# A two-part transformer step on one core: the mixing layer's modulation, spatial mix and output product rebuilt in turned form

## The reference, cut to what matters

```python
def modulate(x, g, shift, scale):
    return rmsnorm(x, g) * (1 + scale) + shift

    sh1, sc1, gt1, sh2, sc2, gt2 = adaln(c, w_mod, b_mod)    # silu(c) @ w_mod + b_mod, six vectors of 1024
    csh1, csc1, ... = adaln(c_ctx, w_mod, b_mod)
    hl, hc = modulate(xl, g_mix, sh1, sc1), modulate(xc, g_mix, csh1, csc1)
    # 8 query heads of 64 in 2 groups (q_gain, rotation), keys and values of both hl and hc: 256 x 512 scores a head
    # spatial gating: u, vv = split(gelu(h @ w_gm)); vv = rmsnorm(vv); w_s is 8 groups of 128 x 128 over rows
    mixed = einsum('gij,bcjgd->bcigd', w_s, vv) + b_s.T[:, :, None];  return u * mixed
    xl_new = xl + gt1 * (concat([attention, gating]) @ w_out)
    xl_new = xl_new + gt2 * expert_choice_ffn(modulate(xl_new, g_ffn, sh2, sc2), w_router, w1, w3, w2)
```

## Time and profile before

| | us |
|---|---|
| executions of the kernel, median of 3 | 1479.61 (1477.10 to 1479.96) |
| profiled execution, its own time | 1483.23 |
| its span, first to last instruction | 1481.4 |
| busy: PE, DVE, ACT, POOL | 1009.3, 333.3, 249.5, 131.7 |
| HBM read, mean rate | 479.66 MB, 324 GB/s over the span |
| granted TensorE clock, mean | 0.845 |

### The profile page before, as it was taken

The page is one execution under the profiler, slowest core; times in us unless marked ns, Lnnn a source line. Parts: engine busy times, 40 slices in busy tenths (PEclk is TensorE's granted clock), DMA queues, the critical chain, the costliest instruction groups (busy, mean ns, idle before and its releaser), DMA issues.

```text
span 1481.4 us, 14254 instructions
## 1 busy us (share of the span) xinstructions
PE 1009.3 (68%) x6208; PEld 497.8 (34%) x6208; DVE 333.3 (23%) x749; ACT 249.5 (17%) x511; POOL 131.7 (9%) x102
## 2 busy tenths in 40 slices
PE   4979857665656556566565565656666688789976
PEld 1855642221211111111111111111111687679875
DVE  3854440000010000000000000000000648445561
ACT  2532311000000000000000000000000645434451
POOL 1320300000100000000000000000000462300032
PEclk9989779989877888787888887787878899889988
DMA  9856358999999999999999999999999141234401
GB/s 386 302 217 226 150 227 334 428 427 428 427 428 429 428 427 428 427 429 428 428 428 427 429 427 428 427 428 428 428 428 423 60 171 58 90 138 158 165 20 43
DMA packets 38340, 481.64 MB, mean 325 GB/s; under 512 B 6577, under 2 KB 7662, under 8 KB 9222
## 3 DMA queue, kind: packets, MB, share of 16 engines
q1 hardware_dynamic: 37126, 476.53, 77.2%
q10 hardware_dynamic: 832, 3.15, 0.5%
q0 software_dynamic: 320, 1.05, 0.2%
HBM read 479.66 MB, written 1.05 MB: 324 GB/s over the span
## 4 chain that ended last, share of the span: by engine, by line
DMA 56%; PE 29%; DVE 8%; ACT 4%; issue 1%; POOL 1%; SPq 0%; DVEq 0%; POOLq 0%; ACTq 0%
DMA ring<-in_t_w 55%; PE PS L466 8%; PE PS L901 4%; PE PS L478 4%; PE PS L947 2%; DMA ring<-in_t_mod 2%; PE PS L456 2%; PE PS L649 1%; ACT S L591 1%; DVE RR L437 1%; PE PS L744 1%; PE PS L835 1%; PE PS L772 1%; ACT RR L431 1%; DVE S L606 1%
## 5 line engine op out<-in xcount | busy, mean ns | idle before, releaser
L901 PE MATMUL PS<-ring,S 128*32 128x512 f32 x2048 | 316.2, 750 | 224.9 <-DMA ring<-in_t_w 223.4
L947 PE MATMUL PS<-ring,S 128*32 128x512 f32 x1024 | 174.9, 817 | 114.2 <-DMA ring<-in_t_w 108.3
L901 PEld LDWEIGHTS PS<-ring,S 128*32 128x32 f32 x2048 | 62.6, 124 | 468.0 <-DMA ring<-in_t_w 346.5
L466 PE MATMUL PS<-RR,SR 128*128 128x512 f32 (+3 forms) x520 | 144.0, 398 | 14.5 <-DVE RR L627 6.6
L437 POOL TENSOR_TENSOR RR<-ring,RR 128x1024 fp32r<-128x1024 f32 (+2 forms) x43 | 94.8, 2232 | 267.9 <-ACT RR L431 267.2
L947 PEld LDWEIGHTS PS<-ring,S 128*32 128x32 f32 x1024 | 33.9, 131 | 238.6 <-DMA ring<-in_t_w 159.2
L466 PEld LDWEIGHTS PS<-RR,SR 128*128 128x128 f32 x520 | 99.9, 197 | 39.8 <-DVE RR L627 7.3
L486 ACT ACTIVATE S<-PS 128x512 f32<-128x512 f32 (+3 forms) x60 | 33.6, 568 | 388.4 <-PE PS L456 338.1
L456 PE MATMUL PS<-KC,S 128*128 128x128 f32 (+1 forms) x378 | 59.8, 309 | 46.5 <-DVE S L1346 13.0
L431 ACT ACTIVATE RR<-ring 128x1024 fp32r<-128x1024 f32 (+3 forms) x95 | 89.2, 1003 | 9.9 <-DMA ring<-in_t_in_kv 6.0
L1699 ACT ACTIVATE S<-PS 128x512 f32<-128x512 f32 x16 | 9.6, 597 | 474.0 <-PE PS L901 474.0
(11 more groups left out here) (275 smaller groups left out, 935.8 us busy)
## 6 DMA issues: line engine op xcount, KB each, us to landing
ring<-in_t_w SPq DMA_DIRECT2D x192, 2048.0 KB, 31.5
ring<-in_t_mod SPq DMA_DIRECT2D x12, 2048.0 KB, 11.2
ring<-in_t_out SPq DMA_DIRECT2D x6, 2048.0 KB, 7.6
ring<-in_t_e_g SPq DMA_DIRECT2D x2, 2048.0 KB, 8.4
ring<-in_t_o_q SPq DMA_DIRECT2D x2, 2048.0 KB, 7.4
ring<-in_t_o_k SPq DMA_DIRECT2D x2, 2048.0 KB, 7.5
ring<-in_t_o_v SPq DMA_DIRECT2D x2, 2048.0 KB, 7.5
ring<-in_t_o_g SPq DMA_DIRECT2D x2, 2048.0 KB, 7.4
```

Source lines behind the costliest of these rows:

```text
L466: m = pe.e.matmul(PS[:, b, 0:width], l_, r_, start=(k == 0 and n == 0), stop=(k == k8 - 1 and n == 2))
L901: m = pe.e.matmul(PS[32 * j:32 * j + 32, b, :], XE[:, 2 * k + kk, 32 * e_:32 * e_ + 32], place[name, e_, k][:, kk, 512 * j:512 * j + 512], ...
L947: m = pe.e.matmul(PS[q:q + 32, b, :], HT[e_ % 2][:, 128 * s + 32 * j:128 * s + 32 * j + 32], place["w2", e_, j][:, s, 512 * dh:512 * dh + ...
```

## The change

- **Modulation by halves.** w_mod is cut in 12 units of one vector's 512 columns (all 1024 rows, eight matmuls). ACT copies the row, four matmuls with a two-column selector turn it (`mod_cols`, L742), and DVE adds bias and gain (`mod_col`). Scale and shift of columns 0 to 511 come first, then kv over those, then scale and shift of the rest, then kv's second half. DVE modulates x and ctx together, with one residue for both; ACT makes both high parts.
- **Ring.** Order: sc1 and sh1 of half 0, kv, sc1 and sh1 of half 1, q, vv, u, six units of gt1, sc2, sh2, w_out in two units, gt2 in two, experts.
- **Attention.** u by `straight`; w_s comes turned from memory and its mixing result turned. Probabilities are divided by their sum on DVE before they are transposed, so that the values stay stationary: eight matmuls of 64 × 256 for two passes. Mixing and attention results go straight to `MT`'s parts. High parts and residues of w_out are made within passes 5 to 8.
- **Router stage.** The output product by `straight`, into x turned (`XT`, 1 MB from memory), gt1 a column scalar; logits from this turned x1 with w_router times the scale; mean squares by matmul; x1 turned back by 16 transposes; both gt2 units ahead of the affinity transposes; the first gather takes one expert, four more follow (`GROUPS`). `g_final` is fetched among the experts.
- **Small inputs.** One transfer of 806 KB instead of 552.5 KB and some twenty small ones and a transpose.

```diff
+MODS = [(n, h) for pair in (("sc1", "sh1"), ("gt1",), ("sc2",), ("sh2",), ("gt2",)) for h in range(2) for n in pair]
...
+    mod_unit("sc1", 0, 0)
+    mod_unit("sh1", 0, 1)
+    in_unit("kv", 256, 2, 2, 2048)
+    mod_unit("sc1", 1, 3)
+    mod_unit("sh1", 1, 4)
+    in_unit("q", 512, 5, 6)
+    in_unit("vv", 512, 0, 1)
+    in_unit("u", 512, 3, 4)
+    for n, slot in zip(MODS[4:10], (2, 5, 6, 0, 1, 2)):
+        mod_unit(*n, slot)
+    for h, slot, hslot in ((0, 5, 6), (1, 3, 4)):
+        unit(("out1", h), unit_rows(f"t_out1_{h}", 8, 512), 8, 512, slot, hslot)
+    mod_unit("gt2", 0, 0)
+    mod_unit("gt2", 1, 1)
+    SLOTS = (2, 5, 6, 3, 4, 0, 1)
...
             if key == ("in", "u"):
-                sp.e.dma_start(wr[:], kview(A["w_router"])).then_inc(*landed("w_router"))
-                sp.e.dma_start(sinkb[:], A["e_sinks_2"].partition_broadcast(P)).then_inc(*landed("sinks"))
-                sp.e.dma_start(bfb[:], A["o_b_f_2"].partition_broadcast(P)).then_inc(*landed("b_f"))
-                sp.e.dma_start(wf[:], kview(A["o_w_in_2"])[:, :, 3072:3088]).then_inc(*landed("wf"))
+                sp.wait_ge(("xn", 0), ("xn", 1))
+                sp.e.dma_start(XT, A["t_xT"].rearrange("p (k t) -> p k t", k=8)).then_inc(*landed("xT"))
...
+        def mod_part(name, h):
+            key, w = ("mod", name, h), place[name, h]
+            b = banks.take(key, ALL6)
+            pe.wait_ge(banks.was[key], ("cv", 0), ("cv", 1), ("load", (name, h)))
+            for k in range(8):
+                q = k % 4
+                m = pe.e.matmul(PS[32 * q:32 * q + 32, b, :], cvec[:, k, :], w[:, k, :], start=k < 4, stop=k >= 4)
+            m.then_inc(*pe.mark(used((name, h)), key))
+        def mod_cols(name, h):
+            key = ("col", name, h)
+            b = banks.take(key, ALL6)
+            pe.wait_ge(banks.was[key], out_of(("mod", name, h)))
+            row = bm[:, MODS.index((name, h)) % 3, :]
+            for s in range(4):
+                m = pe.e.matmul(PS[:, b, 2 * s:2 * s + 2], row[:, 128 * s:128 * s + 128], quarters[:, 0:2], start=True,
+                                stop=True)
+            m.then_inc(*pe.mark(key))
...
+        mod_part("sc1", 0)
         pe.wait_ge(*[("xn", i) for i in range(4)])
         for k in range(8):
             transposes(pe, ("raw", k), ALL6, [(XN if i < 2 else XC)[:, i % 2, 128 * k:128 * k + 128] for i in range(4)])
-        mod_part(0, 2)
-        mod_part(0, 3)
-        mod_cols(0)
+        mod_cols("sc1", 0)
+        mod_part("sh1", 0)
+        mod_cols("sh1", 0)
         for i in range(4):
             banks.take(("kv", i), ALL6, hold=True)
+            pe.wait_ge(banks.was["kv", i])
+        kv_part(range(4))
+        mod_part("sc1", 1)
+        mod_cols("sc1", 1)
+        mod_part("sh1", 1)
+        mod_cols("sh1", 1)
+        kv_part(range(4, 8))
         for i in range(4):
-            pe.wait_ge(banks.was["kv", i])
             banks.release(("kv", i))
-        for k in range(8):
-            pe.wait_ge(("h", k), ("split", ("in", "kv"), k))
-            for i in range(4):
-                for n, (l_, r_) in enumerate(products(("in", "kv"), (HI[:, i // 2], LO[:, i // 2]), k, slice(0, 256),
-                                                      slice(128 * (i % 2), 128 * (i % 2) + 128))):
-                    m = pe.e.matmul(PS[:, banks.of["kv", i], 0:256], l_, r_, start=(k == 0 and n == 0),
-                                    stop=(k == 7 and n == 2))
-        m.then_inc(*pe.mark(("kv", 0), ("kv", 1), ("kv", 2), ("kv", 3), used(("in", "kv"))))
         for i in range(2):
...
+            for n2 in range(2):
+                straight(pe, ("u", n2), ("in", "u"), HL, n2, final=n2 == 1)
                 yield
             for i in range(2):
                 b = banks.take(("mixed", i), ALL6)
-                pe.wait_ge(banks.was["mixed", i], out_of(("wst", 0)), out_of(("wst", 1)), ("vn", 0), ("vn", 1))
+                pe.wait_ge(banks.was["mixed", i], ("load", "w_s"), ("vn", 0), ("vn", 1))
                 for g in range(8):
-                    m = pe.e.matmul(PS[:, b, 64 * g:64 * g + 64], WST[:, g, :], VV[:, i, 64 * g:64 * g + 64], start=True,
-                                    stop=True)
+                    m = pe.e.matmul(PS[64 * (g % 2):64 * (g % 2) + 64, b, 128 * (g // 2):128 * (g // 2) + 128],
+                                    VV[:, i, 64 * g:64 * g + 64], WST[:, g, :], start=True, stop=True)
                 m.then_inc(*pe.mark(("mixed", i)))
                 yield
-            for G in (1, 2):
-                for k in range(4):
-                    mod_part(G, k)
-                    yield
+            for n, part_ in enumerate(A1_MODS):
+                mod_part(*part_)
+                if n:
+                    mod_cols(*A1_MODS[n - 1])
+                yield
+            mod_cols(*A1_MODS[-1])
+            yield
 
...
+                    pe.wait_ge((1, "p", n - 1, g))
...
+            if n and n % 2 == 0:
+                batch, i = n // 2 - 1, (n - 1) // 4
+                if batch % 2 == 0:
+                    banks.take((1, "o", i), (OB[i],))
+                    pe.wait_ge(banks.was[1, "o", i])
+                pe.wait_ge(out_of(("kv", 3)), *[out_of((1, "t", m_, g)) for m_ in (n - 2, n - 1) for g in range(2)])
+                for s in range(4):
+                    for g in range(2):
+                        m = pe.e.matmul(PS[64 * g:64 * g + 64, OB[i], 256 * (batch % 2):256 * (batch % 2) + 256],
+                                        KV[:, s, 128 + 64 * g:192 + 64 * g], PTB[batch % 2][:, s, g, :], start=s == 0,
+                                        stop=s == 3)
+                m.then_inc(*pe.mark((1, "pv", batch), *([(1, "o", i)] if batch % 2 else [])))
         rest(side)
...
+        pe.wait_ge(("mixt", 0), ("mixt", 1), ("MT", 0), ("MT", 1))
+        for n2 in range(4):
+            straight(pe, ("out1", n2), ("out1", n2 // 2), MT, n2 % 2, final=n2 % 2 == 1, ks=(4, 5, 6, 7, 0, 1, 2, 3))
+            if n2:
+                logits(n2 - 1)
+        pe.wait_ge("sqa")
+        mean_square(sqa, True)
+        logits(3)
+        pe.wait_ge(("sq", 3))
+        mean_square(sq2[0], False)
+        for i in range(2):
+            banks.release(("logits", i))
+        for i in range(2):
+            for h in range(2):
+                transposes(pe, ("x1t", i, h), ALL6, [XT[:, 4 * h + k, 128 * i:128 * i + 128] for k in range(4)])
+        mod_part("gt2", 0)
+        mod_part("gt2", 1)
         b = banks.take("affT", ALL6)
...
+        for h in range(2):
+            mod_col("sc1", h)
+            mod_col("sh1", h)
+            for k in range(4 * h, 4 * h + 5):
+                if k < 4 * h + 4:
+                    for r in range(2):
+                        v = RAW[:, r, k, :]
+                        t = dve.e.tensor_scalar(v, v, ab[:, 2 * r, k:k + 1], ab[:, 2 * r + 1, k:k + 1], ALU.mult, ALU.add)
+                    t.then_inc(*dve.mark(("modulated", k)))
+                if k > 4 * h:
+                    dve.wait_ge(("h hi", k - 1))
+                    dve.e.tensor_tensor(LO[:, :, k - 1, :], RAW[:, :, k - 1, :], HI[:, :, k - 1, :].bitcast(F32),
+                                        ALU.subtract).then_inc(*dve.mark(("h", k - 1)))
         lo_all(dve, ("in", "q"))
...
+            for n in range(len(A1_MODS) + 1):
+                if n < 2:
+                    i, c = n, slice(128 * n, 128 * n + 128)
+                    dve.wait_ge(("mixg hi", i))
+                    dve.e.tensor_tensor(MT[1][:, 4:8, c], mixt[i], MT[0][:, 4:8, c].bitcast(F32), ALU.subtract).then_inc(
+                        *dve.mark(("mixt", i)))
+                if n >= 1:
+                    mod_col(*A1_MODS[n - 1])
                 yield
+            for _ in range(2):
+                yield
+            for c in pieces_of(("out1", 1)):
+                lo_piece(dve, ("out1", 1), c)
+                yield
...
+                probabilities_out(dve, n - 1, 1)
+            if n < 8:
+                for g in range(2):
+                    idx = 8 * i + 4 * g + hn
+                    c = slice(idx, idx + 1)
+                    dve.wait_ge((1, "e", n, g))
+                    dve.settle(dve.e.reciprocal(sm1[:, c], sm1[:, c]))
+                    p = PB[(2 * n + g) % 4]
+                    dve.e.tensor_scalar(p, p, sm1[:, c], None, ALU.mult).then_inc(*dve.mark((1, "p", n, g)))
+            turn(side)
+            if n == 5:
+                outputs_low(0)
+        outputs_low(1)
...
+            more = [("out1", h) for h in range(2)]
+            for n in range(len(A1_MODS)):
+                if n < 2:
+                    act.wait_ge(("mixg", n))
+                    act.e.activation(MT[0][:, 4:8, 128 * n:128 * n + 128], mixt[n], ACT.Copy).then_inc(
+                        *act.mark(("mixg hi", n)))
+                mod_row(*A1_MODS[n])
+                yield
+            for u in more:
+                for c in pieces_of(u):
+                    hi_piece(act, u, c)
```

(24 more changed lines are left out.)

546 lines of the change are left out of this document (238 added, 308 removed).

## The result

| | before | after |
|---|---|---|
| median of the executions, us | 1479.10 | 1500.13 (1499.79 to 1501.67) |
| ratio, 95% interval | | 1.0141 (1.0123 to 1.0159) |
| profiled execution, span | 1483.23, 1481.4 | 1500.10, 1498.3 |
| mean granted clock | 0.845 | 0.822 |
| HBM read, MB | 479.66 | 481.21 |

A forecast was written before the change was run, and what follows sets the result against it. It took the start to the first expert matmul, the experts' weight bytes and an unchanged rest to add up; 7.0 − 5.5 + 2.5 + 1.2 = +5.2 us on 1479.61 gave 1484.8, range 1472 to 1493.

The forecast's parts named there:

- Slower: Whole kernel: slower by more than 3 us (0.2%), chance 0.52.
- At nothing: Items said to cost no time, among them the larger consts transfer, the second gather and the ring order.
- Term 1: Mix: modulating by halves makes the query weights' residues start 7.0 us later (+1.5 to +10).
- Term 2: Attention, first scores to start of the output product: 5.5 us shorter (-11.5 to -2.5), turned products costing nothing extra.
- faster: Attention's end: TensorE keeps its upper clock in the last four heads' value matmuls; near 1475 us, chance 0.27.
- Term 3: Router, output product to first expert matmul: 2.5 us longer (-1.2 to +5).
- Term 4: Experts: the last gain's 512 KB, now fetched among them, add 1.2 us, or 0 in a gap.
- A larger loss: Half clock over transposes and both gt2 units, POOL's residues slowing the heads: +9 to +13 us, near 1491, chance 0.08.
- turning not at par: u and output product: two narrow products dearer than one wide, +9 to +11 us, about 1494, chance 0.02.
- ring not full: Weight ring not full when the experts start: +5 us per missing unit, chance 0.01.

The follow-up runs named there:

- e1: Changed kernel, with SyncE waiting until ctx has landed, after consts and the first modulation unit, before issuing the other weights: 1491.25 us, ratio 1.0082.
- e2: Changed kernel with the second half's modulation units and column groups ahead of the kv products on TensorE: 1485.46 us, ratio 1.0041.
- f4: Changed kernel with idle filler matmuls (28, 10 and 5) in three holes at the attention's end: 1497.10 us, ratio 1.012.
- g1: Changed kernel with ctx first, second half's units before kv, gt2 in attention, x1's transposes behind affinities, and 9, 5, 2 filler matmuls: 1464.00 us, ratio 0.990.
- e3: Changed kernel with the two gt2 units moved from the router stage into the attention's seventh pass: 1492.58 us, ratio 1.0097.
- f3: Changed kernel with ctx first, second half's units before kv, gt2 in attention, and the last gain fetched after the last expert unit: 1477.78 us, ratio 0.9989.

## Why the prediction was wrong, point by point

**Which way and why.** Slower was the likeliest case (0.52), and the structure held: a microsecond ahead of the experts moves the last unit by one. The size did not: +21.0 for +5.2. At the last unit, 15.3 later than forecast, the parts are: inputs 8.5, the rest of the mix 3.1, attention −1.3, router 3.7, experts 1.4.

**"At nothing: consts in one larger transfer (SP and DMA have room up to 15 us, TensorE waits for the first unit anyway)" is the step that failed: 8.0 to 8.5 us.** I looked at whom TensorE's first instruction waits for and not at what else used the time: SyncE's row loads kept the weights out of the queues until 4.62, and kv and q until 12.2, while x and ctx were landing. Removing them was a change in the order of all transfers. The row was there to be read, in SyncE's own timeline and in ctx's start-to-landing time. e1 gives back 8.0 of it.

**Term 1, the split modulation: forecast 26.5 us from the start of modulation to the query residues, measured 27.0.** VectorE's hole was to go from 39.6 to 51.0, 11.4 us, and measured 12.8 (48.4 to 61.2); e2 shows it to be TensorE's order alone. Two sizes were short: the transposes took 5.75 (granted clock 0.62; I took 4.6), and the second kv block took 7.50 (clock 0.78), so that the key squares came 1.3 later than the residues' shift says. With ctx's 8.5 these make the 18.6.

**Term 2, attention: −6.8 for −5.5, in its bounds.** The chain through ScalarE came out nearly as worked: a hole of 8.3 us ahead of the seventh pass's values, both last groups at 3.68. The turned products are at par: u took 12.35 for 12.70, gave 0.12 a piece, and the output product at the full clock (f4) takes 11.76 + 5.99 + 5.99 for 22.82, 0.9 more. The rival "faster" named the right deciding point; the values did not run at clock 1.0. What it is worth when they do: from first scores to affinities f4 gains 4.2 with an overrun of 3.7 in it, and g1 gains 4.9.

**Term 3, router: +6.2 for +2.5, beyond its bound of 5.** The affinities came 42.9 behind the output product, not 38.6. 2.5 of these 4.3 are the product's cold start (its first 96 matmuls took 14.25, in f4 11.76), 1.4 the transposes (3.31, I took 1.9), the rest mean squares partly at half clock (1.85 for 1.03). (The term's own sum gives 1.2, not 1.3, ahead of its share for half clock.) Behind the affinities nothing was gained, 17.12 for 17.11, where I had 0.7 for fewer copies. And gt2 was undersized: I counted 3.8 for its units; without them and their copies ahead of the exponentials the router is 7.3 shorter (e3).

**Term 4: +2.6 for +1.2.** 1.7 of it are the first four expert units, 8.91 us for 7.07, at a granted clock of 0.77: SyncE gets the first slot 3.69 behind the first expert matmul, 1.98 before. That leaves 0.9 for the gain's bytes, which no run shows by themselves (f3).

**Rivals.** "A larger loss" (0.08) named half clock in the router, which is part of it, and gave 1491, but the gt2 units in it ran at the full clock (3.64 for two); "turning not at par" and "ring not full" are excluded by the rows (transfers had all landed: TensorE's first wait for the ring comes ahead of the tenth expert unit, as before). The reading of the earlier trace rows is off by one slice: the DMA engines stand at 9 tenths from slice 8, not 7.

## What to carry to other kernels

A small transfer that is taken away also takes away the time its issue held a queue back: list for each early load what is in flight beside it before and after, and hold bulk weights behind the inputs that start the chain. Where work is split in halves to start sooner, put the second half's preparation ahead of the first half's consumers on the engine's list, in the wait that is there anyway. After waits of 2.03, 5.08 and 8.31 us TensorE's next value matmuls took 3.67 or 3.68, about double; short strings behind such waits should be priced so, and the wait can be filled with work that ends before the real work is ready. One profile of each kernel doesn't settle a difference of 4 us ahead of the experts: two profiles of the same code differed by 3.8.
